# Expert weights in a mixture-of-experts loop: the second matrix read in 16,384 B stretches, two matrices as a strided moving operand

## The reference, cut to what matters

```python
def expert_block(args):
    xb, e = args
    return (jax.nn.silu(xb @ w1[e]) * (xb @ w3[e])) @ w2[e]
...
out = jnp.zeros((T + 1, D), jnp.float32).at[row_token].add(row_gate[:, None] * ys.astype(jnp.float32))
```

## Time and profile before

| what | value |
|---|---|
| time, median of 3 runs | 2256.28 us (2253.89 to 2257.93) |
| the profiled execution: its own time, its span | 2254.45 us, 2252.7 us |
| PE busy, share of the span | 1871.4 us, 83% |
| weight loads (PEld) busy | 1266.2 us, 56% |
| DVE, ACT busy | 798.6 us, 694.0 us |
| chain that ended last | PE 57%, DMA 27%, DVE 8%, ACT 4% |
| `ring<-in_w` transfers | 192 of 2048.0 KB, median 19.6 us from issue to landing |
| L1855 (`hidden`) matmul records | 4096, 288.9 us busy, idle before them 112.1 us, most of it for `ring<-in_w` |
| HBM read | 498.03 MB |

### The profile page before, as it was taken

One profiled execution on the slowest core, in us unless ns is written; L12 is line 12 of the kernel. 1 busy time (PEld: TensorE's weight loads), 2 busy tenths in 40 slices (PEclk: granted clock), 3 DMA queues, 4 the chain that ended last, 5 costly groups with the idle time before them and its releaser, 6 DMA issues.

```text
span 2252.7 us, 35882 instructions
## 1 busy us (share of the span) xinstructions
PE 1871.4 (83%) x14468; PEld 1266.2 (56%) x14468; DVE 798.6 (35%) x1526; ACT 694.0 (31%) x1266; POOL 40.8 (2%) x150
## 2 busy tenths in 40 slices
PE   6998998767777777777777777499889799998988
PEld 4775787644343443343443343268456688887876
DVE  4436325342222222222222222742465423332245
ACT  3337422222222222222222222322335422221142
POOL 0000000000000000000000000200000000000000
PEclk9999999979999999999999999799899899999999
DMA  5230121559999999999999999122110223233220
GB/s 155 85 117 15 51 99 56 201 217 426 426 426 427 427 426 426 425 427 428 425 427 426 425 427 415 55 88 65 43 44 29 60 90 104 83 112 112 94 75 38
DMA packets 109572, 501.11 MB, mean 222 GB/s; under 512 B 12856, under 2 KB 60216, under 8 KB 76480
## 3 DMA queue, kind: packets, MB, share of 16 engines
q1 hardware_dynamic: 102880, 491.01, 54.7%
q10 hardware_dynamic: 5952, 7.04, 1.0%
q0 software_dynamic: 672, 2.11, 0.3%
HBM read 498.03 MB, written 2.11 MB: 222 GB/s over the span
## 4 chain that ended last, share of the span: by engine, by line
PE 57%; DMA 27%; DVE 8%; ACT 4%; issue 2%; SPq 1%; ACTq 0%; DVEq 0%; POOLq 0%; POOL 0%
DMA ring<-in_w 26%; PE bank L562 12%; PE bank L563 12%; PE bank L564 12%; PE bank L1855 7%; PE bank L1827 3%; PE bank L1846 3%; DVE w_lo L640 2%; ACT w_hi L631 1%; DMA raw<-in_w_in 1%; PE bank L704 1%; PE bank L557 1%; PE bank L728 1%; PE bank L716 1%; SPq L1528 1%
## 5 line engine op out<-in xcount | busy, mean ns | idle before, releaser
L1855 PE MATMUL bank<-ring,XTs 128*32 128x256 f32 x4096 | 288.9, 430 | 112.1 <-DMA ring<-in_w 111.4
L640 DVE TENSOR_TENSOR w_lo<-raw,w_hi 128x2048 fp32r<-128x2048 f32 (+3 forms) x84 | 184.4, 2196 | 443.9 <-ACT w_hi L631 443.7
L2046 DVE TENSOR_TENSOR x<-x,bank 128x512 f32<-128x512 f32 x264 | 163.9, 682 | 488.5 <-PE bank L1846 488.5
L562 PE MATMUL bank<-hTh,w_hi 128*128 128x512 f32 (+1 forms) x728 | 290.9, 400 | 15.8 <-DVE w_lo L640 12.9
L1855 PEld LDWEIGHTS bank<-ring,XTs 128*32 128x32 f32 x4096 | 143.1, 121 | 259.6 <-issue 201.8
L563 PE MATMUL bank<-hTh,w_lo 128*128 128x512 f32 (+1 forms) x728 | 287.9, 395 | 0.0
L564 PE MATMUL bank<-hTl,w_hi 128*128 128x512 f32 (+1 forms) x728 | 285.4, 392 | 0.0
L631 ACT ACTIVATE w_hi<-raw 128x2048 fp32r<-128x2048 f32 (+3 forms) x84 | 153.8, 1832 | 247.5 <-PE bank L564 239.4
L1864 PE MATMUL bank<-ring,aT 128*32 128x256 f32 x2048 | 123.8, 382 | 89.0 <-DVE aT L2066 89.0
L562 PEld LDWEIGHTS bank<-hTh,w_hi 128*128 128x128 f32 (+1 forms) x728 | 137.1, 188 | 56.6 <-DVE w_lo L640 19.3
L1693 ACT ACTIVATE y<-bank 32x256 f32<-32x256 f32 x256 | 96.1, 376 | 220.7 <-PE bank L1846 136.8
(11 more groups left out here) (356 smaller groups left out, 2258.6 us busy)
## 6 DMA issues: line engine op xcount, KB each, us to landing
ring<-in_w SPq DMA_DIRECT2D x192, 2048.0 KB, 19.6
raw<-in_w_in SPq DMA_DIRECT2D x24, 1024.0 KB, 5.4
raw<-in_w_gate SPq DMA_DIRECT2D x11, 1024.0 KB, 5.3
raw<-in_w_up SPq DMA_DIRECT2D x11, 1024.0 KB, 5.3
raw<-in_w_down SPq DMA_DIRECT2D x11, 1024.0 KB, 4.9
raw<-in_w_out SPq DMA_DIRECT2D x4, 1024.0 KB, 5.0
raw<-in_w_o SPq DMA_DIRECT2D x4, 1024.0 KB, 5.2
raw<-in_w_ple_gate SPq DMA_DIRECT2D x4, 1024.0 KB, 5.0
```

Of the source, the lines that this page charges most:

```text
L562: pe.matmul(dst, left[0], right[0], start=start, stop=False)
L640: v.tensor_tensor(w_lo[:, k % PARTS, 0:size], raw[:, k % RAW, 0:size], w_hi[:, k % PARTS, 0:size].bitcast(F32), ALU.subtract).then_inc(lo_ ...
L1855: mm = pe.matmul(Hb[BLK * j:BLK * (j + 1), :], XTs[u][:, 4 * (c % 2) + 2 * h + c // 2, :], w[:, at_:at_ + Q], start=(h == 0 and c == 0), s ...
L2046: ins = v.tensor_tensor(xs, xs, Sb[t % 2][n][:, :], ALU.add)
```

## The change

1. `w2` is loaded like `w1` and `w3`: partition p takes rows 4p to 4p+3, one stretch of 16,384 B in place of two of 8,192 B.
2. `down` is unchanged. With the new layout the piece (h, r) that it reads holds the rows 4p + 2h + r. The hidden units must come in that order, so `hidden` reads its moving operand with a step: quarters 0 and 2 take the columns 4p and 4p+1 of their matrix, quarters 1 and 3 the columns 4p+2 and 4p+3, each as two runs of 128 values, 16 B apart.
3. `Hs` then is in the right order, and the two transposes read 128 neighbouring values.

```diff
                 w = weights[m][bass.ds(expert, 1), :, :]
                 dst = ring[3 * u + m]
-                if m < 2:
-                    src = w.rearrange("a (p c) n -> p (a c) n", p=P)
-                    dst = dst[:, :].rearrange("p (c n) -> p c n", c=DC)
-                else:
-                    src = w.rearrange("a (h p r) n -> p (a h) (r n)", h=2, p=P)
-                    dst = dst[:, :].rearrange("p (h n) -> p h n", h=2)
+                src = w.rearrange("a (p c) n -> p (a c) n", p=P)
+                dst = dst[:, :].rearrange("p (c n) -> p c n", c=DC if m < 2 else 4)
                 sp.dma_start(dst, src).then_inc(landed[3 * u + m], 16)
...
                         w = ring[3 * u + j // 2]
-                        at_ = 512 * (4 * h + c) + Q * (j % 2)
-                        mm = pe.matmul(Hb[BLK * j:BLK * (j + 1), :], XTs[u][:, 4 * (c % 2) + 2 * h + c // 2, :], w[:, at_:at_ + Q],
+                        w_cols = w[:, 512 * (4 * h + c):512 * (4 * h + c + 1)].rearrange("q (p n) -> q n p", n=4)
+                        mm = pe.matmul(Hb[BLK * j:BLK * (j + 1), :].rearrange("s (r p) -> s r p", r=2),
+                                       XTs[u][:, 4 * (c % 2) + 2 * h + c // 2, :], w_cols[:, 2 * (j % 2):2 * (j % 2) + 2, :],
                                        start=(h == 0 and c == 0), stop=(h == 1 and c == 3))
...
                     for r in range(2):
-                        mm = pe.transpose(Ab[:, P * r:P * (r + 1)], Hs[:, r:Q:2], ident)
+                        mm = pe.transpose(Ab[:, P * r:P * (r + 1)], Hs[:, P * r:P * (r + 1)], ident)
                     mm.then_inc(a_filled, 1)
```

## The result

The changed kernel takes 2306.26 us (median of 4 runs, 2305.27 to 2307.4) against 2255.09 us for the kernel before (4 runs): a ratio of 1.0226, 95% interval 1.0208 to 1.0243. It is 51 us slower. The forecast was 2251.5 us.

What follows compares the result with a forecast made beforehand. The prediction took the expert loop to be bound by DMA transfers at 426 GB/s; 4.8 us saved by longer stretches, the other terms at zero or left out, gave 2256.28 - 4.8 = 2251.5 us, range 2249 to 2320 us.

Steps and rivals of the forecast that it cites:

- the room: PE in a pair of blocks of the expert loop: 5.9 us spare, so `hidden` may take up to 1.8 times as long.
- Longer stretches: w2 loads in the expert loop: 8 long packets replace 8 pairs per engine and block, saving 4.8 us.
- Contiguous `Hs`: Transposes' weight loads: 206 ns become like 140 ns, 0.11 us a block on PE, hidden but for 0.1 us, left out.
- The strided moving operand: Records of `hidden`: reading at a step of 16 B was taken to cost zero.
- headroom: Moving operand of `hidden`: columns pass at about half the contiguous weight load's rate, so a half-speed fetch costs nothing.
- Rival A: In `hidden`, fetching a new 16 B line per column doubles the call, + 1.9 us each, 2314 us; chance 0.22.
- Rival B: In `hidden`, four quarters share one reader, calls take 4 times 1.87 us, 2790 us; chance 0.13.
- rival C: w2 transfers: the longer stretch is worth nothing, time 2256 us; chance 0.05.
- zero cost: The forecast case for strided `hidden`: no cost or a hidden one, 2251.5 us; chance 0.58.

Runs made afterwards that it cites:

- experiment 6: Kernel before with w2 in 16,384 B stretches and the step of four values only in the second of a block's two `hidden` calls: ratio 0.9989 (0.9979 to 0.9998).
- `scatter` run: Kernel before with a step of four values in the moving operand of `scatter` alone: 2256.74 us beside 2258.12 us.
- experiment 1: Kernel before with only w2's load changed to 16,384 B stretches, `hidden` and `Hs` read as before: ratio 0.9974 (0.9965 to 0.9983), median 2249.6 us.

## Why the prediction was wrong

*What bounds the kernel, and the room.* Right. The loop ran at the pace of the transfers, and the room of 5.9 us a pair, a factor of 1.8 on `hidden`, is what experiment 6 and the `scatter` run drew on, with 3.8 and 3.7 us a pair, at an unchanged pace.

*Longer stretches, 4.8 us.* Right alone (experiment 1: 5.9 us, 3.8 to 7.9; 0.15 us a pair in the traces, where the prediction has 2 x 0.078), and worth nothing in the changed kernel, where TensorE is the bound.

*Contiguous `Hs`.* Right: the weight loads went from 206 ns to 141:

```profile
L1895 PEld LDWEIGHTS bank<-cst,Hs x128: 137/141/143, 487.8 to 1460.8; 128*128 128x128 f32 x128
```

*The strided moving operand: the step that failed.* The prediction put this term at zero because "there is headroom for a fetch at half speed". The runs show + 1.9 us a call, four calls a pair, which is beyond the room. Two things were wrong in the reasoning. The weight load of the earlier trace rows slows at a step of two, where a moving operand hardly does (2.01 against 1.93 us): it was a row of the same engine, but of another path, and said nothing of a step of four. And the headroom isn't there: the runs show a factor of two on float32 and on rounded float32 alike, as if a record of float32, which takes twice as long for its columns, also read them twice. That last is an inference; that the slower pace of float32 hides nothing is measured. The row that was held to be too far, VectorE's, 2.0 ns against 1.12, had the right sign and nearly the right factor (1.8), though it is another engine at another step.

*Rival A* is what happened: every column on a line of its own (that the line is what counts stays an inference), `hidden` doubled, TensorE the bound, no waits for weights, a DMA share under 1. It was priced at 2314 us. Measured are 2306. The loop, from its first `hidden` to its last `down`, is 475.97 to 1403.78 us before and 476.04 to 1462.18 after, + 58.3 us, against + 57.5 in the prediction. That the two are so near is in part luck. A pair gained 1.35 us, not 1.6, and 2 pairs, in which the granted clock fell to 0.50 for a short while, were 1.65 us longer. The second pair gained 3.8 us, not 1.6 (27.10 us before, 30.88 after), for before it had less to wait than the later ones. The stretch from the last pair's first `hidden` to the last `down` gained 5.3 us, not 1.6 (1382.98 to 1403.78 before, 1436.11 to 1462.18 after). What the prediction missed besides lies behind the loop:

```profile
476.04:1462.18 986.14, 888.23 (x9023) 378.14 (x9024) 247.82 (x572) 256.38 (x537) 21.01 (x124) 1.00 0.97 399
1462.18:2305.60 843.42, 751.01 (x3338) 579.79 (x3338) 350.04 (x475) 275.44 (x406) 12.11 (x4) 0.95 0.22 72
```
```profile
475.97:1403.78 927.81, 716.89 (x9023) 376.24 (x9024) 247.83 (x572) 255.83 (x536) 21.00 (x124) 0.92 1.00 422
1403.78:2252.70 848.92, 752.42 (x3338) 580.72 (x3338) 349.75 (x475) 276.04 (x406) 12.11 (x4) 0.94 0.23 74
```

The first fence is the changed kernel, the second the one before. The rest of the program is 5.5 us shorter. ScalarE splits the first weights of the second block (L631) before it copies the last results out (L1693 before, L1689 after), and these weights stand in the queue behind the experts'. Before, they came late: the last `scatter` waited 7.01 us for that copy. After, the DMA engines were through in time, and it waited 2.83. The kernel before, then the changed one:

```profile
1406.07 1.91 ACT L631 ACTIVATE w_hi<-raw 128x2048 fp32r<-128x2048 f32 x1 [2.85 <-DMA raw<-in_w_in]
1409.08 1.91 ACT L631 ACTIVATE w_hi<-raw 128x2048 fp32r<-128x2048 f32 x1 [1.10 <-DMA raw<-in_w_in]
1411.01 1.57 ACT L1693 ACTIVATE y<-bank 32x256 f32<-32x256 f32 x4
1412.72 4.77 PE L1846 MATMUL bank<-y,g 64*128 64x512 f32 x12 [7.01 <-ACT y L1693]
```
```profile
1461.50 3.71 ACT L631 ACTIVATE w_hi<-raw 128x2048 fp32r<-128x2048 f32 x2
1465.24 1.57 ACT L1689 ACTIVATE y<-bank 32x256 f32<-32x256 f32 x4
1466.94 1.99 PE L1842 MATMUL bank<-y,g 64*128 64x512 f32 x8 [2.83 <-ACT y L1689]
```

4.2 of the 5.5 us are this wait; it is a reading of the two timelines and was not tried by itself. Where the other 1.3 us come from is open.

*Rival B* (a shared reader) fell with one strided quarter, *rival C* with the stretches alone.

*The chances and the range.* A had 0.22 and zero cost 0.58, on one row of the wrong path. Two rows spoke of strided reads, both of them of a slowdown, and the Trainium skill's rule of the 16 B line too; only the argument of headroom stood against them. The range of 2249 to 2320 us holds the measured time only because it was drawn wide enough for rival A. The forecast itself was a gain, and by its own last line, wrong if over 2256 us, it failed.

## What to carry to other kernels

Keep a float32 moving operand of TensorE at a step of at most two values: in these runs 8 B cost 4%, 12 B half as much again, 16 and 32 B twice the time. A step of four was tried in quarters and in the full array and cost the same factor; the others in quarters alone. If an order has to be made, split it between the operands (a step of two here, a step of two in a small transpose) or put it into the smallest product. Before counting a cost as hidden, work out the factor from which it shows (1.8 here), look for the places where nothing covers it (the first pairs and the last), and ask whether the nearest row measures the same path.

## What the runs showed of the hardware that was not expected

- The factor of two at a step of four does not depend on how fast the columns pass: 0.23 to 0.46 us for 512 columns of rounded float32, and 1.93 to 3.8 us for 8 groups of 256 float32 columns.
- The weight load and the moving operand differ: at a step of two values two weight loads take 0.31 us in place of 0.20, a moving operand loses 4%.
- One slow quarter of the array costs the whole call: 3.90 us, where four slow ones take 3.8.
- Where TensorE hardly waits, the granted clock still fell to 0.50 now and then: in 2 pairs of the changed kernel's loop, in 8 with one strided quarter. Each fall cost 1.6 us (32.8 us for a pair in place of 31.2 in the run with one strided quarter).
